# Router logits and sums of squares moved into the gated unit of a two-layer trunk, with the norm's scale applied per token

## Chip, cores, metric

One core of one Trainium2 chip. The metric is the device time of one execution in microseconds (us). The kernel before takes 1699.36 us, the median of three runs (1696.70, 1699.36 and 1702.51).

## What is computed

The program is a trunk of two residual layers over 256 tokens of width 1024, in float32. Layer 0 is an RWKV-7 mixer and a dense gated unit. Layer 1 is a state-space mixer whose last step is a gated linear unit (`w_glu`), and then a mixture of 8 experts, of which each token takes two. The change lies between the gated linear unit of layer 1 and the first expert:

```python
z = y @ w_glu + b_glu
h = h + z[..., :dim] * sigmoid(z[..., dim:])
hn = h * rsqrt(mean(h * h) + 1e-6) * g          # rmsnorm, g = norm_ffn[1]
logits = hn @ router                            # 8 logits per token
top_val, top_idx = top_k(logits, 2)
gates = softmax(top_val)
out = sum of gate * (silu(hn @ w_gate[e]) * (hn @ w_up[e])) @ w_down[e]
```

The factor `rsqrt(mean(h * h) + 1e-6)` is one number per token. It can therefore be applied after the product with the router, and it doesn't change which two logits are the largest.

## The kernel before

Activations lie with channels on the 128 partitions: HT is [128, 8 chunks, 256 tokens], and chunk k holds channels 128k to 128k+127. Every engine runs its own instruction list in order; they wait for each other by named semaphores.

**The gated unit (NGLU = 8 turns).** TensorE computes in turn t one chunk of both halves of z (`glu_part`, L1134), into bank 4 + t % 4 of PSUM. Turns 0 to 3 have half of their products done earlier; turns 4 to 7 do all sixteen matmuls. Then ScalarE takes the sigmoid (GSG), VectorE multiplies (GHF) and adds to HT, and ScalarE squares the new chunk (SQG). After turn t, TensorE adds the squares of turn t - 1 over the channels by one matmul with a matrix of ones (`norm_part`, L642).

**The norm.** `root(3)` (L355) and `norm(3, ...)` (L1285 to L1291) take root and reciprocal over 128x256 and write the eight chunks of HN.

**The router.** TensorE computes the logits of both halves of the tokens from HN (L1167, 16 matmuls) and turns HN to tokens on partitions (L1172, 16 transposes); ScalarE copies these to XTOK (L574). VectorE finds the two largest logits and their places with a chain of instructions on 128x8 values, each of which waits for the one before (`link`); one loop body is run for each half of the tokens (L1665 to L1674). TensorE counts each expert's tokens (L1177 to L1181). The gates (L1681 to L1686) and the slots POS (L1690 to L1692) follow, and `one_hot` (L1696 to L1698) makes the selection matrix SEL. `gather(0)` (L1216) multiplies XTOK by SEL, and `gathered(0)` (L580, L1734) splits the result into a rounded part XGH and a rest XGL.

**The experts.** There are 8 blocks of at most 128 tokens here, one per expert, each of NP = 14 pairs of hidden chunks. For pair p TensorE runs `gate_up` (L1191, 24 matmuls of 512 columns, with the two transposes of pair p - 1 in the middle, L1197) and then `down` (L1208, 12 matmuls) of pair p - 1. Each product is made of three, from a rounded part and a rest of the weights. ScalarE makes the rounded part (`hi_a` L563, `hi_b` L567), VectorE the rest (`lo_a` L1650, `lo_b` L1656), into rings that hold the next pairs. In `step(b, p)` VectorE does in order: the product MHF of pair p (L1725), two `lo_a` of pair p + 2, the rest MHL of pair p (L1730), for which `down` of pair p waits, and two `lo_b` of pair p + 1. `blocks_in_order` (L1708 to L1721) works out on VectorE which blocks a last loop has to run; in the kernel before it stands after step(0, 0).

**The queue.** SyncE issues the expert weights in order (`load_block`). The first seven transfers go out during the gated unit. The eighth waits for `gate_up` of pair 0, and the ninth stands behind it.

Of the kernel before, what the change touches and what calls it, by code (L numbers as in the profile page):

```python
# [79 lines left out]
def build(nc, xT, prm_d, con_d, wsq, wffn, wglu, wmoe, lora1_d, lora2_d, s5p_d, s5b_d, s5c_d, rout_d, out_d):  # L80
    with ExitStack() as ctx:
# [132 lines left out]
        SQE = at("SQE", [P, KC, T], F32, r(100))  # L214
        RT = at("RT", [P, 2, 16, 16], F32, r(109))
# [64 lines left out]
        def _(sp):  # L280
# [39 lines left out]
            def load_block(b, ex, first=False):  # L320
                for p in range(NP + 1):
# [21 lines left out]
            for n, h in enumerate(halves):  # L343
                sp.wait_ge(S("n_out"), 32 + 4 * (n + 1))
# [4 lines left out]
        def _(act):  # L349
# [206 lines left out]
            for t in range(NGLU):  # L556
                act.wait_ge(S("glu_used"), t + 1)
                act.activation(GSG[:, t % 4, :], half(4 + t % 4, 1), ACT.Sigmoid, bias=prm("glu_b", t)).then_inc(S("g_sig"), 1)
                act.wait_ge(S("h_out"), 6 + t + 1)
                square(3, SQG, slice(t, t + 1))  # L560
# [8 lines left out]
            root(3)  # L569
            hi_a(0, 0)  # L570
            hi_a(0, 1)
            for b in range(2):
                act.wait_ge(S("xt_ps"), b + 1)
                act.activation(XTOK[:, b, :], flat(PS[:, 2 * b:2 * b + 2, :]), ACT.Copy).then_inc(S("xt_sb"), 1)  # L574
            act.wait_ge(S("mask"), 2)
            act.activation(RT[:, :, 7, 0:1], RT[:, :, 6, 0:1], ACT.Exp).then_inc(S("gate_exp"), 1)

            def gathered(b):
                act.wait_ge(S("xg_ps"), b + 1)
# [58 lines left out]
        def _(pe):  # L638
            def norm_part(n, sq, part, start, stop, per=1):
                pe.wait_ge(S("sq"), (0, 2, 6, 8, 16)[n] + part + 1)  # L640
# [496 lines left out]

            pe.wait_ge(S("bt_sb"), 18)
# [12 lines left out]
            for t in range(NGLU):  # L1151
# [12 lines left out]
            pe.wait_ge(S("rout_in"), 16)  # L1164
            for b in range(2):
                for k in range(KC):
                    mm = pe.matmul(PS[:, 4, 8 * b:8 * b + 8], HN[:, k, b * P:(b + 1) * P], ROUT[:, k, :],  # L1167
                                   start=k == 0, stop=k == KC - 1)
                mm.then_inc(S("logits"), 1)
            for b in range(2):  # L1170
                for k in range(KC):
                    tr = pe.transpose(PS[:, 2 * b + k // 4, k % 4 * P:(k % 4 + 1) * P], HN[:, k, b * P:(b + 1) * P], ident)  # L1172
                tr.then_inc(S("xt_ps"), 1)
# [38 lines left out]
            def gather(b):  # L1212
                pe.wait_ge(S("sel"), 3 * b + 3)
# [692 lines left out]
```

## Time and profile before

| | us |
|---|---|
| median of three runs | 1699.36 |
| the profiled execution | 1699.75 |
| its span, first to last instruction | 1697.9 |
| TensorE busy in the span | 1607.5 (95%) |
| VectorE busy | 1257.5 (74%) |
| ScalarE busy | 942.0 (55%) |
| mean granted clock of TensorE, share of full speed | 0.968 |

The span is 1.85 us shorter than the profiled execution's time. Times in the rows below count from the start of the span. "Busy" of TensorE is no measure of its speed: its matmuls overlap, and a matmul that runs at half the clock is busy for longer. Where the pace of matmuls matters, the starts of successive rows are compared.

### The profile page before, as it was taken

The page shows a single profiled execution, that of the slowest core. Times are in us where ns is not written, and L with a number is a line of the kernel's source. Part 1 is how long each engine was busy: PE and PEld are TensorE (multiplying, and loading weights), DVE is VectorE, ACT ScalarE, POOL GpSimd, SP SyncE. Part 2 cuts the span into 40 slices and gives each one's busy share as a digit, 9 for nine tenths or more (in the row PEclk, how much of TensorE's full clock was granted, in tenths as well). Part 3 has the DMA queues.
Part 4 walks back from the last instruction along what each step waited for, and adds up shares of the span by engine and source line. Part 5 has one row for each costly group of instructions (what it writes and reads, how often), then busy time and mean ns, then how long its engine had stood idle before and what let it go on. Part 6 is the DMA issues. An engine that isn't in the chain of part 4 may idle for free.

```text
span 1697.9 us, 28219 instructions
## 1 busy us (share of the span) xinstructions
PE 1607.5 (95%) x12266; PEld 1378.8 (81%) x12266; DVE 1257.5 (74%) x1430; ACT 942.0 (55%) x1028; POOL 83.9 (5%) x69
## 2 busy tenths in 40 slices
PE   5999789899998996999999999999999999999996
PEld 5788787799998885788888888888888888888885
DVE  6255434597782815898998998998988988988884
ACT  1332211476542013676776777777777677677772
POOL 0003400200000800000000000000000000000000
PEclk8999998899997897999999999999999999999998
DMA  7230000454444060599799799799799799799790
GB/s 309 81 110 16 5 4 27 151 190 170 160 152 199 3 273 1 223 367 410 273 374 417 276 374 411 281 375 411 273 385 410 272 384 402 279 385 401 273 389 27
DMA packets 72636, 421.07 MB, mean 248 GB/s; under 512 B 5040, under 2 KB 5296, under 8 KB 37696
## 3 DMA queue, kind: packets, MB, share of 16 engines
q1 hardware_dynamic: 72160, 418.16, 63.2%
q8 instruction: 97, 1.59, 0.4%
q0 software_dynamic: 352, 1.10, 0.2%
q14 instruction: 27, 0.22, 0.0%
HBM read 418.19 MB, written 1.05 MB: 247 GB/s over the span
## 4 chain that ended last, share of the span: by engine, by line
PE 91%; DVE 4%; POOL 2%; issue 1%; ACT 1%; DMA 0%; SPq 0%; POOLq 0%; DVEq 0%
PE PS L1191 36%; PE PS L1208 18%; PE PS L1026 11%; PE PS L660 5%; PE PS L1134 2%; PE PS L1011 2%; PE PS L1216 2%; PE PS L1197 1%; PE PS L642 1%; PE PS L806 1%; PE PS L823 1%; PE PS L1100 1%; PE PS L675 1%; PE PS L1234 1%; POOL SPS L1836 1%
## 5 line engine op out<-in xcount | busy, mean ns | idle before, releaser
L1650 DVE TENSOR_TENSOR LOA<-EXA,WH 128x2048 fp32r<-128x2048 f32 x224 | 504.5, 2288 | 87.0 <-ACT WH L563 87.0
L563 ACT ACTIVATE WH<-EXA 128x2048 fp32r<-128x2048 f32 x224 | 416.8, 1910 | 4.3 <-DMA EXA<-in_wmoe 3.9
L1191 PE MATMUL PS<-WH,XGH 128*128 128x512 f32 x896 | 360.8, 403 | 2.4 <-DVE XGL L1734 2.4
L1191 PE MATMUL PS<-WH,XGL 128*128 128x512 f32 x896 | 350.7, 391 | 0.0
L1191 PE MATMUL PS<-LOA,XGH 128*128 128x512 f32 x896 | 350.1, 391 | 0.0
L1656 DVE TENSOR_TENSOR LOB<-EXB,WH 128x1024 fp32r<-128x1024 f32 x224 | 264.2, 1221 | 8.5 <-ACT WH L567 8.5
L567 ACT ACTIVATE WH<-EXB 128x1024 fp32r<-128x1024 f32 x224 | 224.1, 1052 | 0.0
L1191 PEld LDWEIGHTS PS<-WH,XGH 128*128 128x128 f32 x896 | 168.5, 188 | 35.8 <-DVE XGL L1734 4.3
L1191 PEld LDWEIGHTS PS<-WH,XGL 128*128 128x128 f32 x896 | 168.2, 188 | 35.6
L1191 PEld LDWEIGHTS PS<-LOA,XGH 128*128 128x128 f32 x896 | 168.8, 188 | 31.1
L1208 PE MATMUL PS<-WH,MHH 128*128 128x512 f32 x448 | 174.7, 390 | 4.2 <-DVE MHL L1730 4.2
L1208 PE MATMUL PS<-LOB,MHH 128*128 128x512 f32 x448 | 174.5, 389 | 0.0
L1208 PE MATMUL PS<-WH,MHL 128*128 128x512 f32 x448 | 174.4, 389 | 0.0
L589 ACT ACTIVATE MHH<-PS 128x256 fp32r<-128x256 f32 x112 | 43.1, 384 | 218.6 <-PE PS L1197 218.4
L1026 PE MATMUL PS<-FH,WHI 128*128 128x256 f32 x352 | 101.9, 290 | 5.8 <-DVE FL L1471 5.8
L1208 PEld LDWEIGHTS PS<-WH,MHH 128*128 128x128 f32 x448 | 84.1, 188 | 22.3 <-issue 5.2
L1026 PE MATMUL PS<-FL,WHI 128*128 128x256 f32 x352 | 100.8, 286 | 0.0
L1026 PE MATMUL PS<-FH,WLO 128*128 128x256 f32 x352 | 100.8, 286 | 0.0
L1208 PEld LDWEIGHTS PS<-WH,MHL 128*128 128x128 f32 x448 | 84.1, 188 | 17.5
L1208 PEld LDWEIGHTS PS<-LOB,MHH 128*128 128x128 f32 x448 | 84.2, 188 | 17.1
L1026 PEld LDWEIGHTS PS<-FH,WHI 128*128 128x128 f32 x352 | 68.7, 195 | 6.4 <-issue 6.4
L584 ACT ACTIVATE MSG<-PS 128x256 f32<-128x256 f32 x112 | 43.2, 385 | 53.5 <-PE PS L1191 53.5
(370 smaller groups left out, 2352.7 us busy)
## 6 DMA issues: line engine op xcount, KB each, us to landing
EXA<-in_wmoe SPq DMA_DIRECT2D x112, 2048.0 KB, 8.6
EXB<-in_wmoe SPq DMA_DIRECT2D x112, 1024.0 KB, 8.3
FRA<-in_wffn SPq DMA_DIRECT2D x22, 1024.0 KB, 5.8
RING<-in_wsq SPq DMA_DIRECT2D x16, 1024.0 KB, 4.8
FRB<-in_wffn SPq DMA_DIRECT2D x22, 512.0 KB, 3.8
GLUW<-in_wglu SPq DMA_DIRECT2D x8, 1024.0 KB, 12.4
LORA<-in_lora SPq DMA_DIRECT2D x1, 1536.0 KB, 22.2
LORA<-in_lora SPq DMA_DIRECT2D x1, 1152.0 KB, 19.1
```

What stands on the lines that cost most here:

```text
L563: act.activation(WH[:, n % 4, 0:NARROW], EXA[PAIR_SLOT[n // 2]][:, n % 2, :], ACT.Copy).then_inc(S("m_ahi"), 1)
L567: act.activation(WH[:, n % 4, NARROW:WIDE], EXB[PAIR_SLOT[n // 2]][:, n % 2, :], ACT.Copy).then_inc(S("m_bhi"), 1)
L584: act.activation(MSG[:, :, :], PS[:, p % 2, :].rearrange("p (e t) -> p e t", e=2)[:, :, 0:P], ACT.Silu)\
L589: act.activation(flat(MHH[:, :, :]), PS[:, 4, 0:2 * P], ACT.Copy).then_inc(S("m_hh"), 1)
L660: mm = pe.matmul(out, w[:, h * D + k * P:h * D + (k + 1) * P], x[:, k, :], start=k == 0, stop=k == KC - 1)
L1011: mm = pe.matmul(half(W_BANK[t - 12], h), w[:, h * D + k * P:h * D + (k + 1) * P], T1[:, k, :], start=k == 0, stop=k == KC - 1)
L1026: mm = pe.matmul(out, a, b, start=start and k == 0 and n == 0, stop=stop and k == k_count - 1 and n == 2, skip_group_check=True)
L1134: mm = pe.matmul(half(4 + t % 4, h), GLUW[:, t, h * D + k * P:h * D + (k + 1) * P], HN[:, k, :], start=first and h == 0 and k == chunks[0] ...
L1191: mm = pe.matmul(PS[:, p % 2, :], x[:, k, :], w, start=k == 0 and m == 0, stop=k == KC - 1 and m == 2)
L1208: mm = pe.matmul(PS[:, 2 + c, :], x[:, e, :], w, start=p == 0 and e == 0 and m == 0, stop=p % NP == NP - 1 and e == 1 and m == 2, skip_gro ...
L1650: tt(LOA[slot][:, n % 2, :], EXA[slot][:, n % 2, :], WH[:, n % 4, 0:NARROW].bitcast(F32), ALU.subtract)\
L1656: tt(LOB[slot][:, n % 2, :], EXB[slot][:, n % 2, :], WH[:, n % 4, NARROW:WIDE].bitcast(F32), ALU.subtract)\
```

## The change

The norm over 128x256 is gone, with its root, its reciprocal and the eight chunks of HN. In each turn VectorE now also writes HG, the chunk of HT times g. TensorE's `route_part` (two matmuls of 8 columns, weights from HG) and `square_part` (two of 1 column, weights from SQG) replace the one matmul with ones, with logits and sums of squares by token. The last square is done by VectorE. The scale per token is then made from 128x2 values; it multiplies the turned tokens in the copy to XTOK and the difference of the two largest logits ahead of Exp.

The chain of the router handles both halves of the tokens in most instructions at once, and the slots are made ahead of the gates. The transposes take HG in place of HN, and seven of them stand ahead of the last `route_part`. `hi_a`, `hi_b`, `lo_a` and `lo_b` of the first chunks move into turns 4 to 6, and those of chunk 3's first part behind the gather. The first gather is handed over in two halves, and `blocks_in_order` moves from behind step(0, 0) to behind step(0, 5). On the queue, the ninth transfer (`load_b` of pair 3) waits for the last turn of the gated unit in place of the transposes. Cut to what matters here:

```diff
+        HG = at("HG", [P, KC, T], F32, r(80))
...
-                            sp.wait_ge(S("xt_ps"), 2)
+                            sp.wait_ge(S("glu_used"), NGLU)
...
-                act.wait_ge(S("h_out"), 6 + t + 1)
-                square(3, SQG, slice(t, t + 1))
...
-            root(3)
-            hi_a(0, 0)
-            hi_a(0, 1)
+                if t < NGLU - 1:
+                    act.wait_ge(S("h_out"), 6 + t + 1)
+                    square(3, SQG, slice(t, t + 1))
+                if t in (4, 5):
+                    hi_a(0, t - 4)
+                    hi_b(0, t - 4)
+                elif t == 6:
+                    hi_a(0, 2)
+            act.activation(RT[:, 0, 14, 0:1], ones[:, 0:1], ACT.Sqrt)
+            act.wait_ge(S("n_var"), 4)
+            act.activation(RT[:, :, 12, 0:1], RT[:, :, 12, 0:1], ACT.Sqrt).then_inc(S("n_std"), 1)
+            act.wait_ge(S("t_rstd"), 1)
             for b in range(2):
                 act.wait_ge(S("xt_ps"), b + 1)
-                act.activation(XTOK[:, b, :], flat(PS[:, 2 * b:2 * b + 2, :]), ACT.Copy).then_inc(S("xt_sb"), 1)
-            act.wait_ge(S("mask"), 2)
+                act.activation(XTOK[:, b, :], flat(PS[:, 1 + 3 * b:3 + 3 * b, :]), ACT.Copy, scale=RT[:, b, 13, 0:1])\
+                   .then_inc(S("xt_sb"), 1)
+            act.wait_ge(S("gdiff"), 1)
             act.activation(RT[:, :, 7, 0:1], RT[:, :, 6, 0:1], ACT.Exp).then_inc(S("gate_exp"), 1)
...
-            hi_a(0, 2)
+            act.wait_ge(S("xg_ps"), 1)
+            act.activation(flat(XGH[:, halves[0], :]), PS[:, 5, :], ACT.Copy).then_inc(S("xg_hi"), 1)
+            act.wait_ge(S("xg_ps"), 2)
+            act.activation(flat(XGH[:, halves[1], :]), PS[:, 6, :], ACT.Copy).then_inc(S("xg_hi"), 1)
             hi_a(0, 3)
-            gathered(0)
-            hi_b(0, 0)
-            hi_b(0, 1)
...
+            def route_part(k):
+                if k == 0:
+                    pe.wait_ge(S("rout_in"), 16)
+                pe.wait_ge(S("hg"), k + 1)
+                for b in range(2):
+                    mm = pe.matmul(PS[:, 0, 8 * b:8 * b + 8], HG[:, k, b * P:(b + 1) * P], ROUT[:, k, :],
+                                   start=k == 0 and b == 0, stop=k == KC - 1, skip_group_check=True)
+                return mm
+
+            def square_part(k):
+                if k < KC - 1:
+                    pe.wait_ge(S("sq"), 8 + k + 1)
+                else:
+                    pe.wait_ge(S("last_sq"), 1)
+                for b in range(2):
+                    mm = pe.matmul(PS[:, 3, b:b + 1], SQG[:, k, b * P:(b + 1) * P], ones[:, 0:1],
+                                   start=k == 0 and b == 0, stop=k == KC - 1, skip_group_check=True)
+                return mm
...
                 if t > 0:
-                    norm_part(3, SQG, t - 1, t == 1, False)
-            norm_part(3, SQG, NGLU - 1, False, True)
-
-            pe.wait_ge(S("n_out"), 32)
...
-            for b in range(2):
-                for k in range(KC):
-                    mm = pe.matmul(PS[:, 4, 8 * b:8 * b + 8], HN[:, k, b * P:(b + 1) * P], ROUT[:, k, :],
...
-            for b in range(2):
...
-                    tr = pe.transpose(PS[:, 2 * b + k // 4, k % 4 * P:(k % 4 + 1) * P], HN[:, k, b * P:(b + 1) * P], ident)
...
+                    route_part(t - 1)
+                    square_part(t - 1)
...
+            pe.wait_ge(S("g_mul"), 6)
+            turn_tokens(0, range(KC - 1))
+            route_part(NGLU - 1).then_inc(S("logits"), 1)
+            square_part(NGLU - 1).then_inc(S("n_sum"), 1)
+            turn_tokens(0, (KC - 1,)).then_inc(S("xt_ps"), 1)
+            turn_tokens(1, range(KC)).then_inc(S("xt_ps"), 1)
             pe.wait_ge(S("mask"), 1)
-            cum = CON[:, C_CUM:C_CUM + P]
-            m0, m1 = RT[:, 0, 5, 0:8], RT[:, 1, 5, 0:8]
-            pe.matmul(PS[:, 5, 0:8], cum, m0, start=True, stop=True)
-            pe.matmul(PS[:, 5, 8:16], ones, m0, start=True, stop=False)
-            pe.matmul(PS[:, 5, 8:16], cum, m1, start=False, stop=True)
-            pe.matmul(PS[:, 5, 16:24], ones, m0, start=True, stop=False)
-            pe.matmul(PS[:, 5, 16:24], ones, m1, start=False, stop=True).then_inc(S("logits"), 1)
+            cum, m0, m1 = CON[:, C_CUM:C_CUM + P], RT[:, 0, 5, 0:8], RT[:, 1, 5, 0:8]
+            pe.matmul(PS[:, 7, 0:16].rearrange("p (b e) -> p b e", b=2), cum, RT[:, :, 5, 0:8], start=True, stop=True,
+                      skip_group_check=True)
+            pe.matmul(PS[:, 7, 8:16], ones, m0, start=False, stop=True, skip_group_check=True).then_inc(S("logits"), 1)
+            pe.matmul(PS[:, 0, 32:40], ones, m0, start=True, stop=False)
+            pe.matmul(PS[:, 0, 32:40], ones, m1, start=False, stop=True).then_inc(S("logits"), 1)
...
+                    elif k == KC // 2:
+                        pe.wait_ge(S("xg_lo"), 2)
...
                                        SEL[:, n, :], start=n == 0, stop=n == 1)
+                    if isinstance(b, int) and b == 0 and k == KC // 2 - 1:
+                        mm.then_inc(S("xg_ps"), 1)
                 mm.then_inc(S("xg_ps"), 1)
 
...
+                pe.wait_ge(S("sel"), 3 * b + 3)
...
+                pe.wait_ge(S("xg_lo"), 1 if first else b + 2)
...
             pe.wait_ge(S("xt_sb"), 2)
+            gather(0)
             pe.wait_ge(S("pos"), 1)
-            gather(0)
...
-            norm(3, "ffn1", HN[:, :, :])
-            lo_a(0, 0)
-            lo_a(0, 1)
...
+                dve.wait_ge(S("h_out"), 6 + t + 1)
+                ts(HG[:, t, :], HT[:, t, :], prm("ffn1", t), None, ALU.mult).then_inc(S("hg"), 1)
+                if t in (4, 5):
+                    lo_a(0, t - 4)
+                    lo_b(0, t - 4)
+                elif t == 6:
+                    lo_a(0, 2)
+            tt(SQG[:, NGLU - 1, :], HT[:, NGLU - 1, :], HT[:, NGLU - 1, :], ALU.mult).then_inc(S("last_sq"), 1)
...
+            dve.wait_ge(S("logits"), 1)
+            link(dve.tensor_copy(both(0), PS[:, 0, 0:16].rearrange("p (b e) -> p b e", b=2)))
+            for b in range(2):
+                link(dve.max(RT[:, b, 1, 0:8], RT[:, b, 0, 0:8]))
+            dve.wait_ge(S("n_sum"), 4)
+            ts(both(12, 1), PS[:, 3, 0:2].rearrange("p (b e) -> p b e", b=2), 1.0 / D, NORM_EPS, ALU.mult, ALU.add)\
+                .then_inc(S("n_var"), 1)
+            for b in range(2):
+                link(dve.max_index(IDX[:, b, :], RT[:, b, 1, 0:8], RT[:, b, 0, 0:8]))
+            link(dve.tensor_copy(both(2), IDX[:, :, :]))
+            dve.wait_ge(S("n_std"), 4)
+            dve.reciprocal(both(13, 1), both(12, 1)).then_inc(S("t_rstd"), 1)
+            link(tt(both(3), iota8, wide(2, 0), ALU.is_equal))
+            link(tt(both(4), iota8, wide(2, 1), ALU.is_equal))
+            tt(both(5), both(3), both(4), ALU.add).then_inc(S("mask"), 1)
+            link(tt(both(6, 1), RT[:, :, 1, 1:2], both(1, 1), ALU.subtract))
+            dve.wait_ge(S("t_rstd"), 1)
+            tt(both(6, 1), both(6, 1), both(13, 1), ALU.mult).then_inc(S("gdiff"), 1)
+            dve.wait_ge(S("mask"), 1)
...
-            iota8 = CON[:, C_E8:C_E8 + 8]
-            link(dve.tensor_copy(RT[:, :, 0, 0:8], PS[:, 4, 0:16].rearrange("p (b e) -> p b e", b=2)))
...
-                link(ts(q(3), iota8, RT[:, b, 2, 0:1], None, ALU.is_equal))
-                link(ts(q(4), iota8, RT[:, b, 2, 1:2], None, ALU.is_equal))
-                link(tt(q(6, 1), RT[:, b, 1, 1:2], RT[:, b, 1, 0:1], ALU.subtract))
-                link(tt(q(5), q(3), q(4), ALU.add))
-            dve.memset(GCOL[:, :, :], 0.0).then_inc(S("mask"), 1)
-            dve.wait_ge(S("mask"), 1)
-            dve.memset(GCOL[:, :, :], 0.0).then_inc(S("mask"), 1)
+            link(stt(POS[:, :, 0:8], PS[:, 7, 0:16].rearrange("p (b e) -> p b e", b=2), 1.0, both(5), ALU.add, ALU.mult))
...
+            def slots(col):
+                for n in range(2):
+                    ts(SEL[:, n, :], iota1, POS[:, n, bass.ds(col, 1)], None, ALU.is_equal).then_inc(S("sel"), 1)
...
+            slots(0)
+            v = lambda n, w=8: OV[0:1, n, 0:w]
+            dve.wait_ge(S("logits"), 3)
+            ts(v(0), PS[0:1, 0, 32:40], float(P), None, ALU.is_gt).then_inc(S("pos"), 1)
+            link(ts(POS[:, :, 8:16], POS[:, :, 0:8], -float(P), None, ALU.add))
             dve.wait_ge(S("gate_exp"), 1)
...
-            def one_hot(col):
...
-            dve.wait_ge(S("pos"), 1)
-            one_hot(0)
-            lo_a(0, 2)
-            lo_a(0, 3)
...
+            link(ts(both(8, 1), both(7, 1), 1.0, None, ALU.add))
+            link(dve.reciprocal(both(8, 1), both(8, 1)))
+            link(tt(both(9, 1), both(8, 1), both(7, 1), ALU.mult))
+            link(tt(both(10), both(3), wide(8), ALU.mult))
+            link(tt(both(11), both(4), wide(9), ALU.mult))
+            link(tt(GAT[:, :, 0:8], both(10), both(11), ALU.add))
+            link(dve.tensor_copy(GAT[:, :, 8:16], GAT[:, :, 0:8]))
+            slot_gates(0)
...
-                    if p == 0 and first:
+                    if p == 5 and first:
+                        dve.wait_ge(S("pos"), 1)
                         blocks_in_order()
...
-            gathered(0)
-            lo_b(0, 0)
-            lo_b(0, 1)
+            dve.wait_ge(S("xg_hi"), 1)
+            tt(flat(XGL[:, halves[0], :]), PS[:, 5, :], flat(XGH[:, halves[0], :]).bitcast(F32), ALU.subtract)\
+                .then_inc(S("xg_lo"), 1)
+            dve.wait_ge(S("xg_hi"), 2)
+            tt(flat(XGL[:, halves[1], :]), PS[:, 6, :], flat(XGH[:, halves[1], :]).bitcast(F32), ALU.subtract)\
+                .then_inc(S("xg_lo"), 1)
+            lo_a(0, 3)
```

## Rows read from the trace of the kernel before

**Rows 1.** Busy time of each engine by stretch: PE, PEld, DVE, ACT, POOL, clock, DMA share, GB/s.

```profile
820.00:940.00 120.00, 119.90 (x564) 99.08 (x563) 105.44 (x90) 86.26 (x85) 0.00 (x0) 1.00 0.90 354
```

**Rows 2.** The chain that ended last, in order of time: start, length, what.

```profile
623.64 0.43 PE PS L642 x2
624.07 6.91 PE PS L1134 x32
...
645.69 0.48 ACT GSG L558
...
647.17 0.42 ACT SQG L351
...
654.46 6.99 PE PS L1167 x32
...
672.31 5.22 PE PS L1216 x32
...
678.61 1.24 DVE XGL L1734
679.89 5.75 PE PS L1191 x24
...
703.63 3.00 PE PS L1208 x12
```

**Rows 3.** TensorE in order of time, full clock: small matmuls between large ones.

```profile
715.13 0.50 PE L1224 MATMUL PS<-GCOL,SEL 128*128 128x1 f32 x4
...
715.81 0.39 PE L1191 MATMUL PS<-LOA,XGH 128*128 128x512 f32 x1
```

**Rows 4.** VectorE in order of time: small steps of the router.

```profile
661.49 0.17 DVE L1665 COPY RT<-PS 128x16 f32<-128x16 f32 x1 [2.68 <-PE PS L1167]
...
662.17 0.17 DVE L1670 CAST RT<-IDX 128x8 f32<-128x8 uint32 x1
```

**Rows 5.** Groups of instructions over the whole run: busy us, mean ns, idle before.

```profile
L1539 DVE TENSOR_SCALAR COS<-COS 128x256 f32<-128x256 f32 x8 | 2.4, 295 | 0.3
L563 ACT ACTIVATE WH<-EXA 128x2048 fp32r<-128x2048 f32 x224 | 416.8, 1910 | 4.3 <-DMA EXA<-in_wmoe 3.9
L554 ACT ACTIVATE HN<-PS 128x512 f32<-128x512 f32 x4 | 2.4, 598 | 64.3 <-PE PS L1124 64.3
L600 ACT ACTIVATE OH<-PS,GSL 128x1024 fp32r<-128x1024 f32 x7 | 7.8, 1117 | 3.7 <-PE PS L1208 3.7
L576 ACT ACT_TABLE_LOAD x1 | 1.3, 1283 | 0.0
```

**Rows 6.** Stretches of a quarter us at the clock's changes, columns as in Rows 1.

```profile
651.25:651.50 0.25, 0.00 (x0) 0.00 (x0) 0.25 (x1) 0.25 (x1) 0.00 (x0) 0.69 0.00 0
...
665.00:665.25 0.25, 0.18 (x2) 0.18 (x2) 0.08 (x2) 0.25 (x1) 0.00 (x0) 1.00 0.00 0
...
668.25:668.50 0.25, 0.00 (x0) 0.00 (x0) 0.21 (x2) 0.25 (x1) 0.00 (x0) 0.82 0.00 0
...
675.00:675.25 0.25, 0.25 (x4) 0.25 (x3) 0.25 (x1) 0.00 (x0) 0.00 (x0) 0.52 0.00 0
```

**Rows 7.** The chain that ended last, a later gather at full clock.

```profile
791.50 3.57 PE PS L1216 x32
```

**Rows 8.** TensorE and VectorE in order of time: the second pair's start and `blocks_in_order`.

```profile
692.86 0.47 PE L1208 MATMUL PS<-WH,MHH 128*128 128x512 f32 x1 [1.54 <-DVE MHL L1730]
...
694.89 0.16 DVE L1708 TENSOR_TENSOR_SCAN OV<-CON,OV 1x8 f32<-1x8 f32 x1
...
698.35 0.40 DVE L1725 TENSOR_TENSOR MHF<-MSG,PS 128x256 f32<-128x256 f32 x1
```

**Rows 9.** VectorE in a settled pair of block 0, in order of time.

```profile
747.64 0.41 DVE L1725 TENSOR_TENSOR MHF<-MSG,PS 128x256 f32<-128x256 f32 x1
748.97 4.49 DVE L1650 TENSOR_TENSOR LOA<-EXA,WH 128x2048 fp32r<-128x2048 f32 x2 [0.92 <-ACT WH L563]
```

**Rows 10.** The chain that ended last: TensorE in the same pair.

```profile
755.12 2.72 PE PS L1208 x12
```

More of the change, by code:

```diff
@@ L343, in _ @@
             for n, h in enumerate(halves):
-                sp.wait_ge(S("n_out"), 32 + 4 * (n + 1))
+                sp.wait_ge(S("n_out"), 24 + 4 * (n + 1))
                 sp.dma_start(out_d[:, h, :], HN[:, h, :]).then_inc(S("out_sent"), 16)
@@ L1179, in _, with turn_tokens @@
-            pe.matmul(PS[:, 5, 8:16], cum, m1, start=False, stop=True)
-            pe.matmul(PS[:, 5, 16:24], ones, m0, start=True, stop=False)
-            pe.matmul(PS[:, 5, 16:24], ones, m1, start=False, stop=True).then_inc(S("logits"), 1)
+                    route_part(t - 1)
+                    square_part(t - 1)
+            def turn_tokens(b, chunks):
+                for k in chunks:
+                    tr = pe.transpose(PS[:, 1 + 3 * b + k // 4, k % 4 * P:(k % 4 + 1) * P], HG[:, k, b * P:(b + 1) * P], ident)
+                return tr
@@ L1212, in gather @@
             def gather(b):
-                pe.wait_ge(S("sel"), 3 * b + 3)
+                pe.wait_ge(S("sel"), 3 * b + 2)
                 for k in range(KC):
@@ L1638, in _ @@
                     rotate(n + 1)
-            for t in range(NGLU):
-                dve.wait_ge(S("g_sig"), t + 1)
-                stt(GHF[:, t % 4, :], half(4 + t % 4, 0), prm("glu_a", t), GSG[:, t % 4, :], ALU.add, ALU.mult).then_inc(S("g_mul"), 1)
-                dve.wait_ge(S("g_mul"), t + 1)
-                tt(HT[:, t, :], HT[:, t, :], GHF[:, t % 4, :], ALU.add).then_inc(S("h_out"), 1)
-            dve.wait_ge(S("h_out"), 6 + NGLU)
             def lo_a(b, n):
@@ L1675, in _ @@
-            dve.memset(GCOL[:, :, :], 0.0).then_inc(S("mask"), 1)
-            dve.wait_ge(S("mask"), 1)
-            dve.memset(GCOL[:, :, :], 0.0).then_inc(S("mask"), 1)
-            dve.wait_ge(S("gate_exp"), 1)
-            for b in range(2):
-                q = lambda n, w=8, b=b: RT[:, b, n, 0:w]
-                link(ts(q(8, 1), q(7, 1), 1.0, None, ALU.add))
-                link(dve.reciprocal(q(8, 1), q(8, 1)))
-                link(tt(q(9, 1), q(8, 1), q(7, 1), ALU.mult))
-                link(ts(q(10), q(3), q(8, 1), None, ALU.mult))
-                link(stt(GAT[:, b, 0:8], q(4), q(9, 1), q(10), ALU.mult, ALU.add))
-                link(dve.tensor_copy(GAT[:, b, 8:16], GAT[:, b, 0:8]))
@@ L1687, in _ @@
-            dve.wait_ge(S("logits"), 3)
-            for b in range(2):
-                q = lambda n, w=8, b=b: RT[:, b, n, 0:w]
-                link(stt(q(11), PS[:, 5, 8 * b:8 * b + 8], 1.0, q(5), ALU.add, ALU.mult))
-                link(ts(POS[:, b, 0:8], q(11), -1.0, None, ALU.add))
-                link(ts(POS[:, b, 8:16], POS[:, b, 0:8], -float(P), None, ALU.add))
-            iota = CON[:, C_IOTA:C_IOTA + P]
-            def one_hot(col):
-                dve.tensor_copy(GCOL[:, :, :], GAT[:, :, bass.ds(col, 1)]).then_inc(S("sel"), 1)
-                for n in range(2):
-                    ts(SEL[:, n, :], iota, POS[:, n, bass.ds(col, 1)], None, ALU.is_equal).then_inc(S("sel"), 1)
@@ L1700, in _ @@
-            v = lambda n, w=8: OV[0:1, n, 0:w]
-            ts(v(0), PS[0:1, 5, 16:24], float(P), None, ALU.is_gt).then_inc(S("pos"), 1)
-            dve.wait_ge(S("pos"), 1)
-            one_hot(0)
-            lo_a(0, 2)
-            lo_a(0, 3)
+            for t in range(NGLU):
+                dve.wait_ge(S("g_sig"), t + 1)
+                stt(GHF[:, t % 4, :], half(4 + t % 4, 0), prm("glu_a", t), GSG[:, t % 4, :], ALU.add, ALU.mult).then_inc(S("g_mul"), 1)
+                dve.wait_ge(S("g_mul"), t + 1)
+                tt(HT[:, t, :], HT[:, t, :], GHF[:, t % 4, :], ALU.add).then_inc(S("h_out"), 1)
+                dve.wait_ge(S("h_out"), 6 + t + 1)
[5 more added lines that the diff above has]
+                    lo_a(0, 2)
@@ new lines, in _ @@
+            tt(SQG[:, NGLU - 1, :], HT[:, NGLU - 1, :], HT[:, NGLU - 1, :], ALU.mult).then_inc(S("last_sq"), 1)
+            both = lambda n, w=8: RT[:, :, n, 0:w]
+            wide = lambda n, c=0: RT[:, :, n, c:c + 1].to_broadcast([P, 2, 8])
+            iota8 = CON[:, C_E8:C_E8 + 8].unsqueeze(1).to_broadcast([P, 2, 8])
+            iota1 = CON[:, C_TOK:C_TOK + P]
+            dve.wait_ge(S("logits"), 1)
+            link(dve.tensor_copy(both(0), PS[:, 0, 0:16].rearrange("p (b e) -> p b e", b=2)))
@@ L1769, in step @@
                     dve.wait_ge(S("gsl"), b + 1)
-                    if isinstance(b, int):
-                        one_hot(b + 1)
-                    else:
-                        one_hot(dve.value_load(META[0:1, bass.ds(b + 13, 1)], min_val=0, max_val=2 * NEXP - 1))
+                    col = b + 1 if isinstance(b, int) else \
+                        dve.value_load(META[0:1, bass.ds(b + 13, 1)], min_val=0, max_val=2 * NEXP - 1)
+                    slots(col)
+                    slot_gates(col)
             def steps(b, first, last):
```

25 lines of the change are left out of this document (8 added, 17 removed).

## Prediction

> **What bounds the kernel now.** I read the busy times by stretch first. In the expert blocks TensorE is busy for 119.9 of 120 us at full clock, with the DMA engines at 0.90 [rows 1]. Apart from block 0 the change leaves the work there as it is, so these 900 us or so should stay. The reader then looks in the chain that ended last for the place where it leaves TensorE. That is at 645.69, where the gated unit's last sigmoid starts, and TensorE comes back for good with the first expert matmul at 679.89 [rows 2]. These 34.2 us are a chain without cover: norm, logits, transposes, the router's small steps, gates, slots, gather, split. After it, 23.7 us pass until `down` of pair 1 starts at 703.63 [rows 2], and from there no wait of TensorE shows in block 0. So four intervals decide: the gated unit's turns, the 34.2 us, the first two pairs, and the rest of block 0.
>
> **Turns of the gated unit.** Here TensorE is the bound, so all that is put between two turns counts in full. The matmul with ones that goes took 0.43 us [rows 2]. In its place come eight records (a float32 matmul is two): four of route_part, four of square_part. Four records of one column and the large matmul behind them took 0.68 us from start to start, 715.13 to 715.81 [rows 3]; a large one alone is 2.72 / 12 = 0.23 [rows 10], so the four cost 0.45, of which some 0.1 is the next weights no longer hidden. The router's 8-column records ran at 6.99 / 32 = 0.218 us each [rows 2], at a granted clock of 0.5 up to 665.0 [rows 6]; an estimate for full clock is half, 0.109. Together 4 x 0.109 + 0.45 = 0.89, or 0.46 more than today. Six such places lie ahead of the last sigmoid: **+2.8 us**. Bounds: all eight at 0.085 give +1.5, all eight at 0.218 give +7.9. I take the middle because both rows are of the same kind of instruction with 128x128 weights.
>
> The other engines have room there. VectorE's HG comes 1.8 us after a turn's sigmoid starts (below), against 3.5 us of TensorE work in the shortest turn, half of 6.91 [rows 2]. Turns 4 to 6 last 6.91 + 0.89 = 7.8 us; ScalarE's extra hi_a (1.9) and hi_b (half the elements, 1.0) and VectorE's lo_a and lo_b (2.25 and half of it, 1.1; [rows 5, 9]) end about 7.2 us in, before the next sigmoid. This costs nothing while it stays below 7.8; if that cover went, each us over it would be a us. The weights that they read are issued ahead of turn 2. On SyncE's queue load_b of pair 3 now waits for the last turn, but it stands behind load_a of pair 4, which waits for the first gate_up in both kernels: nothing.
>
> **From the last sigmoid to the first expert matmul.** I count from S, the start of the last sigmoid, now 645.69 + 2.8 = 648.5.
> - HG. VectorE's product and sum end at S+1.48, as today (the square started at 647.17, [rows 2]). The HG instruction, 128x256 with a scalar, is nearest to 0.295 us [rows 5]; S+1.8. The last square on VectorE ends at S+2.25.
> - Logits. TensorE meanwhile does the places of turn 6 and seven transposes (0.89 + 7 x 0.11 = 1.7) and waits for HG. Four small records take 0.50 end to end [rows 3]: logits at S+2.4, sums of squares at S+2.8.
> - Small steps. Copy, maximum and index search for one half took 0.68 us [rows 4], so 0.20 for a step and 0.28 for a search. Copy and two maxima end at S+3.0. The mean (0.2), two searches and the cast (0.75) end at 3.95; reciprocal, two comparisons and their sum give the mask at S+4.75. The root with its table falls beside the searches.
> - Counts and slots. Counting takes 0.50: S+5.3; POS and two SEL (0.2 and 2 x 0.24) end at S+6.0.
> - Turned tokens. XTOK needs the reciprocal (S+4.15) and is two copies of 128x1024 with a scale. Such a copy took 1.117 us [rows 5]: the second ends at S+6.5. This is later than SEL, so ScalarE and not VectorE releases the gather.
> - Gather. Today it took 5.22 us [rows 2], a later one at full clock 3.57 [rows 7]. See the clock, below. I take 5.2: it ends at S+11.7. Its first half ends at S+10.2 with its result, the copy of 128x512 takes 0.6 [rows 5] and the rest half of 1.24 [rows 2]: S+11.45. So TensorE itself is the last, and the first expert matmul starts at **S+11.75**.
> - Gates. Exp with its table load of 1.28 [rows 5] ends at S+8.0, and eight steps of 0.20 at S+9.6. They lie beside the gather.
>
> The interval shrinks from 34.2 to 11.75: **-22.45 us**. About 18 small steps on the path have a bound of 0.15 and 0.26 each, so -0.8 to +1.0; HG between 0.25 and 0.48.
>
> **The clock.** Today the granted clock fell to half at 651.3, when TensorE had little to do after 645.7, and rose at 665.0, behind 10.5 us of small matmuls and transposes that had begun at 654.46. It fell again at 668.4, although ten small records had run since 665.1, and rose at 675.1, 2.8 us into the gather [rows 2, 6]. So small records with pauses did not hold it. In the new kernel S+0 to S+6.5 holds about 2.8 us of small records and transposes. I expect the fall by the start of the gather and a rise inside it as today; that is the 5.2 above.
>
> The Trainium skill ("TensorE: Matmul & The Clock Gate", section "HAM oscillation") says that the clock is lowered when the array is left idle between bursts of matmuls. By that rule alone the clock would hold here, since no pause is longer than about 1.2 us; by the fall at 668.4 it would not. With the rule the sum would be that of the third case below.
>
> **The first two pairs.** Today `down` of pair 0 started at 692.86 after a wait of 1.5 us for MHL [rows 8]. From there 2.72 for it [rows 10] and 5.75 for gate_up of pair 2 [rows 2] would allow 701.33, but `down` of pair 1 started at 703.63. VectorE had spent 694.89 to 698.35 on `blocks_in_order` ahead of the product [rows 8]. Without these 3.46 us MHL is ready near 700.1, and TensorE is the limit: **-2.3 us**. What is late next is lo_a of chunk 3, which now follows the gather: hi_a to S+14.35 and lo_a to S+16.65, against gate_up of pair 1 at S+17.5. That is a cover of 0.85 us. The wait of 1.5 us at pair 0 stays.
>
> **blocks_in_order behind pair 5.** In a settled pair the product starts at 747.64, VectorE then idles for 0.92 us until lo_a, and MHL, as long as the product, ends near 753.8; `down` needs it at 755.12 [rows 9, 10]. Moved by 3.46 us the product starts at 751.1, and MHL is ready after 0.41, 4.49 and 0.42 at about 756.4. What waits is `down`, for **+1.3 us**; the pair after that catches up. Bounds: 0.8 and 2.5.
>
> **The sum.** 1699.75 + 2.8 - 22.45 - 2.3 + 1.3 = 1679.1. The profiled execution was 0.4 above the median, so the predicted median is **1678.7 us**.
>
> **The rivals.**
> - *Third case: the clock holds.* The gather takes 3.57. Its first half is ready at S+8.4 and copied at S+9.05, but VectorE is at the gates until S+9.6 and makes the rest until S+10.2. The first expert matmul starts at S+10.25, 1.5 earlier: 1677.2. For it speaks that pauses are short; against it, the fall at 668.4.
> - *The clock rises late*, only with the expert matmuls: the gather takes 7.0 (1.8 more) and the first 1.5 to 3 us of work of gate_up run at half, 0.8 to 1.5 more: 1682.
> - *Small matmuls don't overlap in the turns* and keep their pace of 0.218: +7.9 in place of +2.8: 1684. Rows 3 speak against it.
> - *The clock falls in the turns* because of the small records, and the change ends slower. The four last turns are about 29 us of TensorE work. At half clock they would take 29 more: 1708. It decides once more than 20.6 us of work runs at half. Against it: eight ninths of a turn are matmuls of 256 columns.
> - *The gain is given back in the experts*, if the weight stream and not TensorE paced them: 1699. The stream's share is 0.90 and ScalarE's idle time for it is 4.3 us over the run [rows 1, 5]; and the eighth transfer moves forward with the first gate_up.
>
> **How the numbers follow.** The forecast (fall, rise in the gather) has 0.50, the clock holding 0.22, the late rise 0.13, the slow small matmuls 0.09, the two that lose the gain 0.03 each. The first four reach from 1675 to 1686 with the bounds of small steps and of the stall behind pair 5, and the runs of the kernel before lie 3 us to either side. I take 1674 to 1685. 0.3% (5.1 us) is about what a measurement of this kernel can tell from no change: faster 0.94, same 0.03, slower 0.03.
>
> **What would show it.** The last four turns at 7.8 us instead of 6.91 + 0.43 = 7.34 (right), or over 8.5 (small matmuls don't overlap). A first expert matmul 11.75 us after the last sigmoid. The clock below 1.0 in the gather. ScalarE's second XTOK as what releases the gather. `down` of pair 1 with no wait, and one wait of 1.3 us behind pair 6. A settled pair that takes other than 2.72 + 5.7 = 8.4 us would make all of this wrong.

## The result and the profile after

The changed kernel takes 1677.59 us (median of four runs, 1675.27 to 1680.88), the one before 1698.05 us in the same comparison. The ratio is 0.9883 with a 95% interval of 0.9866 to 0.9900, so 20 us faster; the forecast was 1678.7 us. The profiled execution took 1675.67 us, its span 1673.9.

The two profiled spans differ by 24.0 us, 3.4 more than the change can claim: the gated unit starts at 601.42 in the one and at 598.00 in the other, and up to there both run the same instructions. In the kernels run below it starts anywhere from 594.99 to 603.86. The intervals below are therefore measured from marks of their own: the first matmul of the unit's turns, the start of the last sigmoid (S), the first expert matmul (X), the second block's gather, and the end of the span.

The chain that ended last in the changed kernel (start, length, what; L1143 is the unit, L1152 and L1162 are route_part and square_part, L1193 the transposes, L1204 to L1208 the counting, L1245 the gather, L1220 and L1237 gate_up and down):

```profile
598.00 7.10 PE PS L1143 x32
...
621.60 0.34 PE PS L1152 x4
621.94 0.44 PE PS L1162 x4
622.38 7.01 PE PS L1143 x32
629.40 0.34 PE PS L1152 x4
...
645.03 0.48 ACT GSG L567
...
646.52 0.36 DVE HG L1690
...
647.54 0.45 PE PS L1162 x4
647.99 2.02 PE PS L1193 x9
650.01 0.32 PE PS L1204 x2
650.33 0.41 PE PS L1206 x2
650.75 0.43 PE PS L1207 x2
651.17 0.43 PE PS L1208 x2
...
651.70 5.22 PE PS L1245 x32
656.92 5.49 PE PS L1220 x24
...
669.63 2.98 PE PS L1237 x12
...
678.33 2.72 PE PS L1237 x12
...
722.39 2.97 PE PS L1237 x12
```

Before, the same chain passed through the norm, 32 router records (6.99 us) and the gather at 672.31 [rows 2]. The reader should see three things. A turn is 629.40 - 621.60 = 7.80 us long. Between the sigmoid at 645.03 and the gather, TensorE itself carries the chain from 646.9 on. And the gather starts 6.67 us behind the sigmoid in place of 26.6.

The first expert matmul, the copies to XTOK and the making of SEL, in order of time on their engines:

```profile
649.22 2.12 ACT L582 ACTIVATE XTOK<-PS,RT 128x1024 f32<-128x1024 f32 x2 [0.62 <-DVE RT L1713]
...
651.07 0.48 DVE L1726 TENSOR_SCALAR SEL<-CON,POS 128x128 f32<-128x128 f32 x2
...
655.17 0.60 ACT L627 ACTIVATE XGH<-PS 128x512 fp32r<-128x512 f32 x1 [2.32 <-PE PS L1245]
655.80 0.69 DVE L1822 TENSOR_TENSOR XGL<-PS,XGH 128x512 fp32r<-128x512 f32 x1 [1.23 <-ACT XGH L627]
...
656.68 0.48 PE L1220 MATMUL PS<-WH,XGH 128*128 128x512 f32 x1
```

The granted clock (the column behind the five engines) at its fall and its rise, in stretches of a quarter us. Before, it fell at 651.3, which is 5.6 us behind the sigmoid, rose at 665.0, fell again at 668.4 and rose inside the gather at 675.2 [rows 6]. In the changed kernel it fell and rose only once:

```profile
647.75:648.00 0.25, 0.25 (x4) 0.25 (x4) 0.18 (x2) 0.00 (x0) 0.00 (x0) 0.67 0.00 0
...
654.50:654.75 0.25, 0.25 (x4) 0.25 (x3) 0.07 (x1) 0.00 (x0) 0.00 (x0) 0.67 0.00 0
```

### The profile page after: what moved, and what is told of

Same layout as the page of the kernel before. It is cut to its first block, busy times and chain, and to the rows that moved or that the text cites. A ratio compares the mean times of both kernels' runs of the same rounds, so it can differ in the third digit from the quotient of the medians.

```text
span 1673.9 us, 28242 instructions
## 1 busy us (share of the span) xinstructions
PE 1599.6 (96%) x12280; PEld 1372.6 (82%) x12280; DVE 1253.4 (75%) x1417; ACT 941.9 (56%) x1029; POOL 83.9 (5%) x69
## 4 chain that ended last, share of the span: by engine, by line
PE 91%; DVE 4%; POOL 2%; issue 1%; ACT 1%; DMA 0%; SPq 0%; POOLq 0%; DVEq 0%
PE PS L1220 36%; PE PS L1237 18%; PE PS L1035 11%; PE PS L669 5%; PE PS L1143 3%; PE PS L1245 2%; PE PS L1020 2%; PE PS L1226 1%; PE PS L815 1%; PE PS L651 1%; PE PS L832 1%; PE PS L684 1%; DVE LOA L1675 1%; PE PS L1109 1%; PE PS L1266 1%
## 5 line engine op out<-in xcount | busy, mean ns | idle before, releaser
L1220 PE MATMUL PS<-WH,XGH 128*128 128x512 f32 x896 | 360.7, 403 | 0.0
L1220 PE MATMUL PS<-WH,XGL 128*128 128x512 f32 x896 | 350.6, 391 | 0.0
L1220 PE MATMUL PS<-LOA,XGH 128*128 128x512 f32 x896 | 349.9, 391 | 0.0
L1220 PEld LDWEIGHTS PS<-WH,XGL 128*128 128x128 f32 x896 | 168.2, 188 | 35.7
L1220 PEld LDWEIGHTS PS<-WH,XGH 128*128 128x128 f32 x896 | 168.4, 188 | 33.3 <-DVE XGL L1773 1.8
L1220 PEld LDWEIGHTS PS<-LOA,XGH 128*128 128x128 f32 x896 | 168.8, 188 | 31.2
L1237 PE MATMUL PS<-WH,MHH 128*128 128x512 f32 x448 | 174.6, 390 | 3.8 <-DVE MHL L1769 3.8
L1237 PE MATMUL PS<-LOB,MHH 128*128 128x512 f32 x448 | 174.4, 389 | 0.0
L1237 PE MATMUL PS<-WH,MHL 128*128 128x512 f32 x448 | 174.3, 389 | 0.0
L1237 PEld LDWEIGHTS PS<-WH,MHH 128*128 128x128 f32 x448 | 84.1, 188 | 22.0 <-issue 4.8
L1237 PEld LDWEIGHTS PS<-WH,MHL 128*128 128x128 f32 x448 | 84.1, 188 | 17.6
L1237 PEld LDWEIGHTS PS<-LOB,MHH 128*128 128x128 f32 x448 | 84.1, 188 | 17.1
```

What stands on the lines that cost most here:

```text
L1220: mm = pe.matmul(PS[:, p % 2, :], x[:, k, :], w, start=k == 0 and m == 0, stop=k == KC - 1 and m == 2)
L1237: mm = pe.matmul(PS[:, 2 + c, :], x[:, e, :], w, start=p == 0 and e == 0 and m == 0, stop=p % NP == NP - 1 and e == 1 and m == 2, skip_gro ...
```

## The experiments

The intervals of all kernels, in us, from the marks above (the turns' first matmul is in the chain of waits of each; "gather" is how long the first gather took; "clock falls, rises after S" counts from the last sigmoid's start; "to 2nd gather" is X to the second block's gather; "whole" is the first of the turns' matmuls to the end of the span). Each row is the one profiled execution of that kernel:

| kernel | turns | S to X | gather | clock falls, rises after S | X to 2nd gather | whole |
|---|---|---|---|---|---|---|
| before | 44.27 | 34.20 | 5.22 | 5.6, 19.3, again 22.7, 29.5 | 111.61 | 1096.5 |
| changed | 47.03 | 11.65 | 5.22 | 2.8, 9.6 | 110.75 | 1075.9 |
| u_tail | 41.68 | 18.04 | 5.14 | 5.7, 15.9 | 110.96 | 1077.1 |
| u_splits | 47.03 | 15.79 | 5.65 | 2.8, 13.0 | 110.71 | 1079.0 |
| u_gates | 47.03 | 16.14 | 6.32 | 5.1, 15.3 | 110.74 | 1080.3 |
| u_whole | 47.03 | 13.28 | 5.46 | 7.7, 11.1 | 110.91 | 1079.4 |
| u_blocks | 47.04 | 11.88 | 5.45 | 3.3, 10.1 | 111.61 | 1076.1 |
| d_route | 49.71 | 11.59 | 5.47 | 7.4, 10.9 | 110.74 | 1078.8 |
| c_fill | 47.03 | 10.37 | 3.73 | never | 110.75 | 1074.5 |
| c_small | 47.04 | 13.70 | 5.60 | 5.3, 12.1 | 110.73 | 1077.9 |
| n_both | 47.04 | 11.86 | 5.43 | 3.3, 10.1 | 108.27 | 1075.3 |
| after_again | 47.03 | 11.69 | 5.26 | 2.9, 9.7 | 110.73 | 1075.9 |
| n_all | 47.04 | 10.36 | 3.73 | never | 108.13 | 1071.8 |

### The router's work behind the turns (u_tail)

```diff
-                if t > 0:
-                    route_part(t - 1)
-                    square_part(t - 1)
...
+            pe.wait_ge(S("hg"), KC - 1)
             turn_tokens(0, range(KC - 1))
+            for t in range(NGLU - 1):
+                route_part(t)
+                square_part(t)
             route_part(NGLU - 1).then_inc(S("logits"), 1)
```

> The changed kernel with the logits and squares of chunks 0 to 6 taken out of the turns and put behind the last one. In the changed kernel the turns take 47.0 us (first unit matmul to the last sigmoid's start) and 11.65 us lie between that sigmoid and the first expert matmul. Theory (each place in the turns costs about 0.9 us of TensorE, and the clock falls when small records replace large ones): turns 6 x 0.9 shorter, 41.7; behind the last sigmoid 7 x 0.9 = 6.2 more small work, of which the wait for HG covers about 1.2, and the part of it behind the clock's fall runs at half, so that 11.65 becomes 19 to 22. Net 2 to 5 us slower. Rival (the clock holds while TensorE has no pause): 11.65 becomes 16.7, net about 0.

Behind the last turn eight places now stand in a row: the seven that were moved, and the last chunk's own. The last five of them in its chain (the rows of L1162 between them are left out):

```profile
599.68 41.64 PE PS L1143 x192
...
644.66 0.45 PE PS L1152 x4
...
645.55 0.45 PE PS L1152 x4
...
646.45 0.45 PE PS L1152 x4
...
647.46 0.86 PE PS L1152 x4
...
649.17 0.86 PE PS L1152 x4
```

The turns came out at 41.68, as the theory has it: six places cost 5.35 us, 0.89 each, and 0.89 is the step from row to row at full clock. Behind the fall, 5.7 us after the sigmoid, the step is 1.71. But the fall came late, so only the last two of the eight places ran at half, and S to X is 18.04, one us below the range. The net is +1.0 us (-5.35 in the turns, +6.39 behind them), outside both forecasts: between the theory (2 to 5) and the rival (0). In the turns the work is paid for at full clock; behind them part of it is covered by the wait for HG, and part of it runs at half.

The rival's condition can be read here too. Before the fall TensorE had no pause at all. Behind the turns it ran seven transposes and then, from 642.1 to the fall at 647.1, nothing but the small records of route_part and square_part (columns as in [rows 1]):

```profile
645.00:647.00 2.00, 2.00 (x20) 2.00 (x20) 0.00 (x0) 0.00 (x0) 0.00 (x0) 1.00 0.00 0
647.00:649.00 2.00, 2.00 (x12) 2.00 (x12) 0.00 (x0) 0.00 (x0) 0.00 (x0) 0.52 0.00 0
```

### The splits out of the turns (u_splits)

```diff
                 ts(HG[:, t, :], HT[:, t, :], prm("ffn1", t), None, ALU.mult).then_inc(S("hg"), 1)
-                if t in (4, 5):
-                    lo_a(0, t - 4)
-                    lo_b(0, t - 4)
-                elif t == 6:
-                    lo_a(0, 2)
...
+            lo_a(0, 0)
+            lo_a(0, 1)
             dve.wait_ge(S("gate_exp"), 1)
...
+            lo_a(0, 2)
             dve.wait_ge(S("xg_hi"), 1)
```

The same is done on ScalarE, with two hi_a ahead of the copies to XTOK; hi_b and lo_b of the first chunks go behind the first gather's split.

> The changed kernel with hi_a, hi_b, lo_a and lo_b of the first chunks back behind the router's steps, as near to their old places as the waits allow. Theory (with the norm gone the old cover is gone too, so the splits would be on the path): two hi_a ahead of XTOK move the gather from 6.7 to about 9.7 us behind the last sigmoid, and lo_a on VectorE delays XGL to about 15.0; first expert matmul at 15.5 to 16.0 in place of 11.65, and 1 to 2 us more by `down` of pair 1; turns unchanged at 47.0. Total 5 to 6 us slower than the changed kernel. Rival (the splits were and are beside other work, the gain is all the norm's): within 1 us.

S to X rose from 11.65 to 15.79, as said, with the gather at 9.22 and the turns at 47.03 unchanged: in the turns the splits cost nothing. Down of pair 1 came 21.65 us behind X as in the changed kernel, so the further 1 to 2 us did not come, and the whole is 3.1 us longer and not 5 to 6. One us of the difference between these 3.1 and the 4.1 of S to X is not the edit's: behind the last block's gather, where both kernels run the same instructions, this execution took 158.0 us and the changed kernel's 159.0. What made it shorter is open. A kernel without this move would have kept some 4 of the 22.5 us to itself.

### Slots behind the gates (u_gates)

```diff
-                pe.wait_ge(S("sel"), 3 * b + 2)
+                pe.wait_ge(S("sel"), 3 if isinstance(b, int) and b == 0 else 3 * b + 2)
...
-            slots(0)
             v = lambda n, w=8: OV[0:1, n, 0:w]
...
             slot_gates(0)
+            slots(0)
```

> The changed kernel with the slots made behind the gates, as before. Theory: SEL waits for Exp, its table load and eight small steps, and is ready about 9.9 to 10.2 us behind the last sigmoid in place of 6.5, so the gather starts 3.4 us later and the first expert matmul comes at 14.5 to 15.2 (less if the clock is up for all of the gather). Rival (the copy to XTOK or the clock is the real limit of the gather's start): below 1 us.

The gather started at 10.06 in place of 6.67 (+3.4, as said). TensorE's waits in that kernel name the cause (who waited for whom: us, times, longest):

```profile
PE PS L1245 <- DVE SEL L1726: 3.8, 1, 3.8
```

S to X is 16.14, a us over the range, because the clock rose only 15.3 us behind the sigmoid and the gather took 6.32. So the order of slots and gates is worth 3.4 us, and the slower gather adds 1.1.

### The first gather handed over whole (u_whole)

```diff
-            act.wait_ge(S("xg_ps"), 1)
+            act.wait_ge(S("xg_ps"), 2)
             act.activation(flat(XGH[:, halves[0], :]), PS[:, 5, :], ACT.Copy).then_inc(S("xg_hi"), 1)
```

> The changed kernel with the first gather's copy waiting for both halves (the two copies and the two subtractions stay two). Theory: the first copy (0.6) and subtraction (0.69) then start behind the gather's end and nothing covers them: first expert matmul 1.4 to 1.6 us later, 13.1 in place of 11.65, with the same gather. Rival (the first expert matmul is bound by something else, as the rest of chunk 3): no change.

X came 13.28 behind the sigmoid (+1.6), and TensorE waited 1.5 us between gather and X. The rival falls. The whole is longer by more than that, 3.5 us; most of the rest is the pace of the later blocks (see n_both).

### blocks_in_order back in pair 0 (u_blocks)

```diff
-                    if p == 5 and first:
+                    if p == 0 and first:
```

> The changed kernel with blocks_in_order back behind step(0, 0). Theory: first expert matmul to `down` of pair 1 takes 23.7 to 24.0 us again in place of 21.65, and the wait of 1.3 us of `down` of pair 6 is gone; net 0.8 to 1.1 us slower. Rival (VectorE would catch up in the first pairs too): 21.65 stays, net 1.3 us faster.

Down of pair 1 came 23.74 us behind X, to the hundredth what it was before, and the second gather 111.61 behind X, again as before, against 110.75: +0.86. The move is worth 0.9 us, of 2.1 gained in pair 1 and 1.2 lost at pair 6. The rival, that VectorE would catch up in the first pairs too, falls.

### route_part twice (d_route)

```diff
                     route_part(t - 1)
+                    for b in range(2):
+                        pe.matmul(PS[:, 0, 64 + 8 * b:72 + 8 * b], HG[:, t - 1, b * P:(b + 1) * P], ROUT[:, t - 1, :],
+                                  start=False, stop=True, skip_group_check=True)
                     square_part(t - 1)
```

> The changed kernel with the two 8-column matmuls of route_part done twice in each turn, the second time into unused columns. Prices the disputed size by itself. Theory (half of the pace at half clock, 0.109 a record): 4 x 0.109 = 0.44 us per turn, the turns 47.0 to 49.7. Rival (no overlap, 0.218 a record or the 0.25 us that a single record lasts): 0.87 to 1.0 per turn, 52.3 to 53. Behind the last sigmoid nothing changes but for the clock.

The turns grew from 47.03 to 49.71: 2.68 / 6 = 0.447 for four records, or 0.112 each. The estimate from the half clock (0.109) holds and the rival's 0.218 falls.

### Filling TensorE's pauses with large and with small matmuls (c_fill, c_small)

```diff
+            def filler(n):
+                for _ in range(n):
+                    pe.matmul(half(6, 0), ones, HN[:, 0, :], start=True, stop=True)
...
             turn_tokens(0, range(KC - 1))
+            filler(1)
...
             turn_tokens(1, range(KC)).then_inc(S("xt_ps"), 1)
+            filler(3)
...
+            filler(2)
             pe.wait_ge(S("xt_sb"), 2)
```

In the second kernel the filler is `pe.matmul(PS[:, 6, 0:8], ones, HN[:, 0, 0:8], ...)`, and there are 2, 6 and 4 of them.

> The changed kernel with six matmuls of 256 columns that nobody reads: one behind the first seven transposes, three behind the last transposes (TensorE otherwise waits for the mask), two ahead of the gather. Theory (the clock fell 2.8 us behind the last sigmoid, although TensorE had no pause over 0.33 us, because the matmuls were small and the transposes few): the granted clock stays at or returns to full for most of the gather, which then takes 3.6 to 4.5 us in place of 5.2; first expert matmul at 10.5 to 11.5. Rival (the fall is due to the pause or can't be bought back this way, and the fillers stand in the way of the counting): 11.9 to 12.9.

> As the kernel with the fillers of 256 columns, but the fillers have 8 columns and are twice as many, so that TensorE's pauses are filled for the same time. With the large fillers the granted clock stayed at 1.0 from the last sigmoid to the first expert matmul; in eight kernels without them it fell 2.75 to 7.75 us behind the sigmoid. Theory (what lowers the clock is that the matmuls are small, not that TensorE pauses): the clock falls as without fillers, the gather takes 5.0 to 6.3 us, first expert matmul at 11.6 to 13.5. Rival (the clock falls when the array is left idle between bursts): it stays at 1.0, the gather takes 3.6 to 3.8 us, first expert matmul at 10.3 to 10.6.

Two stretches of each, first of the large fillers (the sigmoid at 650.89), then of the small ones (650.78); columns as in [rows 1]:

```profile
655.00:657.00 2.00, 2.00 (x15) 1.87 (x14) 1.03 (x8) 1.92 (x2) 0.00 (x0) 1.00 0.00 0
657.00:659.00 2.00, 2.00 (x16) 1.90 (x15) 0.64 (x5) 1.69 (x3) 0.00 (x0) 1.00 0.00 0
```

```profile
655.00:657.00 2.00, 2.00 (x17) 2.00 (x16) 0.76 (x5) 2.00 (x2) 0.00 (x0) 0.76 0.00 0
657.00:659.00 2.00, 2.00 (x11) 2.00 (x11) 0.98 (x6) 1.57 (x3) 0.00 (x0) 0.50 0.00 0
```

TensorE is busy throughout in both, and neither trace has a pause of it between the last sigmoid and the gather. With the large fillers the clock stayed up, the gather took 3.73 us and X came at 10.37, 1.3 earlier, just under the forecast of 10.5 to 11.5. With the small ones the clock fell 5.3 us behind the sigmoid. So in this kernel it falls without any pause between TensorE's records, as in u_tail. What it is in the small records that doesn't hold the clock, the traces don't say. The small fillers also cost more: at half clock they took longer than the pauses they filled, the gather started at 8.34, and X came at 13.70, just over the range.

### Two stalls of the first block, and all together (n_both, after_again, n_all)

```diff
                 product(b, p)
+                if first and 5 <= p < 10:
+                    if p == 5:
+                        dve.wait_ge(S("pos"), 1)
+                    for one in ordering[4 * (p - 5):4 * (p - 4)]:
+                        one()
...
+                if first and p == 0:
+                    turned(b, p)
                 if more_a:
                     lo_a(after(b, p + 2)[0], 2 * after(b, p + 2)[1] + 1)
-                turned(b, p)
+                if not (first and p == 0):
+                    turned(b, p)
```

`ordering` holds the instructions of `blocks_in_order` one by one. n_all has the fillers of 256 columns as well.

> The changed kernel with blocks_in_order cut into pieces of four instructions, one behind the product of each of pairs 5 to 9, where VectorE idles 0.9 us, and with MHL of pair 0 ahead of the second lo_a. Theory: `down` of pair 6 no longer waits (-1.3), `down` of pair 0 waits 1.5 us less (-1.5): 2.5 to 2.8 us less from the first expert matmul to the end. Rival (ScalarE's second hi_a, not VectorE's order, holds MHL of pair 0): only the 1.3.

> The changed kernel unaltered, beside the next one on the same chip. Turns 47.1, the last sigmoid to the first expert matmul 11.4 to 13.0 depending on where the clock falls and rises, from there to the second block's gather 110.75; 1675 to 1681 us.

> The changed kernel with the pieces of blocks_in_order, MHL of pair 0 moved ahead, and the fillers of 256 columns together. Theory (the three savings lie in different intervals and add up): turns 47.1, then 10.4 to the first expert matmul (-1.3), then 108.3 to the second block's gather (-2.5); 3.8 us less than the changed kernel up to there. Rival (the later blocks' slower pace that came with the pieces, 124.85 in place of 124.61 us a block, is caused by them): 1.5 us of it are given back over the other blocks and the gain at the end is 2 to 2.5 us; if the pace belongs to the execution, n_all may well show 124.6.

Both stalls went: down of pair 1 comes 20.27 behind X (-1.4) and the second gather 108.27 (-2.5). Yet the whole is only 0.6 us shorter, since each later block took 124.85 to 124.90 us and not 124.61, and S to X was 0.2 longer (11.86). The same 124.86 stands in u_whole, whose blocks weren't touched, and n_all, which has the same edit as n_both, ran at 124.61. The pace thus doesn't follow the edit; each kernel was profiled once, so whether it changes from execution to execution of one kernel isn't shown, and what sets it stays open. Its 0.24 us a block lie in gate_up alone (77.27 against 77.02 us in the chain of one block; down has 38.11 in both).

In n_all the savings add up. From its chain:

```profile
602.70 7.10 PE PS L1143 x32
...
656.78 3.57 PE PS L1251 x32
660.35 5.49 PE PS L1226 x24
...
680.40 3.00 PE PS L1243 x12
```

The whole is 1071.8 against 1075.9 in after_again: 4.1 us less, 3.8 expected. In device time n_all takes 1671.83 us (median of five, 1670.07 to 1676.33), the changed kernel on the same chip 1676.11 (median of six, 1673.69 to 1679.56), the kernel before 1696.40. The ranges of the two overlap. In the profiled executions the start of the program alone differs by 4.0 us, as much as the gain (the unit starts at 602.70 in n_all and at 598.71 in after_again). Against the kernel before their ratios are 0.9843 (0.9817 to 0.9869) and 0.9867 (0.9843 to 0.9890). The traces carry the difference, the times alone would not.

## Why the prediction held, point by point

| term | forecast | measured |
|---|---|---|
| turns | +2.8 | 47.03 - 44.27 = +2.8 |
| last sigmoid to first expert matmul | 34.2 to 11.75 | 34.20 to 11.65 |
| first two pairs | -2.3 | 23.74 to 21.65 = -2.1 |
| blocks_in_order behind pair 5 | +1.3 | with the last: 111.61 to 110.75 = -0.9, so +1.2 |
| sum | -20.65 | 1096.5 to 1075.9 = -20.6 |

**Turns.** The price of a place came from two kinds of rows, [rows 3] for one column and half of the half-clock pace [rows 2] for eight. Turns of 7.80 us bear out the sum, d_route the eight columns. The chain shows where the exposed weight load went: 7.01 for the large matmuls in place of 6.91.

**The small steps.** Logits were copied at S+2.55 (2.4 forecast), the mask was ready at S+4.64 (4.75), the copies to XTOK began at S+4.19 (4.2), Exp ended at S+7.8 (8.0), XGL at S+11.46 (11.45).

**What was wrong: the gather's release.** The prediction names ScalarE's second XTOK. It ended at 651.34, 0.2 before the forecast, SEL at 651.55, and TensorE's own counting matmuls, which stand ahead of the gather, left the array at 651.60. The step that failed is "Counting takes 0.50: S+5.3": it assumed the full clock. The clock was already at half, so a pair of records took 0.43 and not 0.22, POS began at S+5.83, and SEL was 0.5 late. The gather began at S+6.67 and not 6.5. Three releasers within 0.3 us made the error harmless.

Two runs show that the rest of this step was right. In u_whole and d_route the clock fell only at S+7.7 and S+7.4, behind the counting. POS then began at S+5.42 and S+5.43 (5.3 forecast), and the gather at S+6.35 and S+6.37, released as forecast. From u_whole (sigmoid at 643.30):

```profile
649.65 5.46 PE L1245 MATMUL PS<-SEL,XTOK 128*128 128x128 f32 x32 [0.60 <-ACT XTOK L582]
```

**The clock.** The fall by the start of the gather and the rise inside it were right. What the prediction left out is that the fall could come as early as 2.8 us behind the sigmoid and so slow the counting. Over the eleven profiled executions without large fillers, the one before the change among them, it came anywhere from 2.8 to 7.7 us behind the sigmoid, and the gather took 5.14 to 6.32. That it took 5.22 us here, to the hundredth what the kernel before had, is partly luck: the prediction had no reason for the moment of the rise but that it had come 2.9 us into the gather before (675.2 - 672.3), and it came 3.0 us into it here (654.7 - 651.7). In the three other executions with the same code up to X (after_again, u_blocks, n_both) S to X was 11.69, 11.88 and 11.86. The weight against the rule of the Trainium skill ("TensorE: Matmul & The Clock Gate", section "HAM oscillation", that idling between bursts lowers the clock) was right in this kernel: TensorE's longest pause before the fall was 0.33 us, and in u_tail and c_small the fall came with no pause at all. By that rule the clock would have held; here the measurement decides.

**The first two pairs.** The wait for `blocks_in_order` was the cause, as u_blocks shows. The term was over-sized by 0.2: it counted 2.72 for `down` of pair 0, but behind its wait this `down` took 2.98, as the chain shows at 669.63. The wait of 1.5 us of pair 0 stayed as said; n_both shows that it was VectorE's order, and it could be taken away.

**The rivals.** Nothing was given back in the experts: X to the end is 1018.0 before and 1017.2 after. The small matmuls didn't keep their pace of 0.218 in the turns (0.112 in d_route). The clock held at 1.0 in all of the last turns.

## What to carry to other kernels

A scale per row that commutes with what follows can leave a serial chain: here this let logits and sums start inside a stage that TensorE already bounds, for 0.46 us a turn, and took 22.5 us off a chain that nothing covered. But when the chain is cut, what it covered comes into the open: the splits (4 us), the order of slots and gates (3.4 us) and the handing over in halves (1.6 us) are worth 9 of these 22.5 us when undone one at a time. The other 13.5 are put down to the norm and the logits by subtraction; no run puts the norm back by itself. So list what stands beside a chain before shortening it. And where only a chain of one engine's small steps is left, price TensorE's few matmuls between them at both clocks: the counting ran at half in the changed kernel and at full in u_whole and d_route, a difference of 0.3 us at the gather.

## What the runs showed of the hardware

- The granted clock fell from 1.0 to 0.5 while TensorE ran without a pause: in u_tail 5.7 us behind the last sigmoid, behind five us of small records alone, and in c_small 5.3 us behind it, with fillers of 8 columns. With six fillers of 256 columns in the same pauses it held in both kernels that had them (c_fill, n_all). That is worth 1.3 us here (11.65 to 10.37), for work whose result nobody reads.
- A float32 matmul of 8 columns with new 128x128 weights costs 0.22 us at full clock (0.447 / 2 in d_route) and 0.43 at half (the chain at 650.75), of one column not measurably less (0.44 us for two at L1162); the large matmul behind such a row took 0.1 us more (7.01 in place of 6.91 for the turn's 32 records).
- A settled expert block took 124.60 to 124.65 us in most executions, 124.85 to 124.90 in n_both and 124.84 to 124.87 in u_whole; one block of d_route took 124.99. In the block compared above the excess lies in gate_up. No edit goes with it.
- Of the difference between single executions of one kernel, several us lie in stages that no edit here touches: the same code reached the gated unit between 594.99 and 603.86.
